# Fifteen matmuls of ones, results unread, in three waits of TensorE ahead of the experts

## The reference

```python
def moe_swiglu(h, w_router, w1, w3, w2):
    logits = (h @ w_router).astype(jnp.float32)
    top_val, top_idx = lax.top_k(logits, TOP_K)          # 2 of 8 experts for each token
    probs = jax.nn.softmax(top_val, axis=-1)
    combine = jnp.sum(jax.nn.one_hot(top_idx, N_EXPERTS, dtype=jnp.float32) * probs[..., None], axis=-2)
    out = jnp.zeros_like(h)
    for e in range(N_EXPERTS):                           # 1024 -> 3584 -> 1024 each
        out = out + combine[..., e:e + 1] * swiglu(h, w1[e], w3[e], w2[e])
    return out
```

## Time and profile before

| | |
|---|---|
| three timed runs | median 2060.42 us, 2057.94 to 2065.71 |
| the profiled execution | 2065.84 us |
| its span, first to last instruction | 2064.0 us (1.84 us lie around it) |
| TensorE busy | 2024.1 us, 98% of the span |
| weight loads busy | 1729.1 us, 84% |
| VectorE, ScalarE busy | 1580.3 us (77%), 1249.8 us (61%) |
| chain that ended last | TensorE 91%, VectorE 5%, issue 2%, ScalarE 2% |
| mean granted TensorE clock | 0.991 |

### The profile page before, as it was taken

One profiled execution on the slowest core, in us unless ns is written; L12 is line 12 of the kernel. 1 busy time (PEld: TensorE's weight loads), 2 busy tenths in 40 slices (PEclk: granted clock), 3 DMA queues, 4 the chain that ended last, 5 costly groups with the idle time before them and its releaser, 6 DMA issues.

```text
span 2064.0 us, 28723 instructions
## 1 busy us (share of the span) xinstructions
PE 2024.1 (98%) x10749; PEld 1729.1 (84%) x10749; DVE 1580.3 (77%) x1218; ACT 1249.8 (61%) x1066; POOL 13.9 (1%) x21
## 2 busy tenths in 40 slices
PE   9999999999999999999999999999999999999998
PEld 8988878789998988888777888888888888888887
DVE  4777955765445777955767898898989889898987
ACT  4665455444334565455446777777777777777775
POOL 0000000000000000000000000000000000000000
PEclk9999999999999999999999999999999999999999
DMA  7532455345554532455348999999999999999996
GB/s 257 165 100 90 142 176 183 102 155 188 187 184 143 184 103 82 143 166 182 104 170 296 380 354 379 372 357 379 358 381 354 378 371 355 379 358 379 356 375 243
DMA packets 240765, 516.59 MB, mean 250 GB/s; under 512 B 11528, under 2 KB 34312, under 8 KB 240686
## 3 DMA queue, kind: packets, MB, share of 16 engines
q1 hardware_dynamic: 238274, 507.39, 69.4%
q0 software_dynamic: 2144, 7.88, 1.1%
q10 hardware_dynamic: 268, 0.22, 0.0%
HBM read 513.35 MB, written 2.12 MB: 250 GB/s over the span
## 4 chain that ended last, share of the span: by engine, by line
PE 91%; DVE 5%; issue 2%; ACT 2%; DVEq 0%; ACTq 0%
PE PS L480 27%; PE PS L482 26%; PE PS L481 26%; PE PS L564 7%; PE PS L1085 1%; ACT hi L1208 1%; PE PS L1048 1%; PE PS L802 1%; PE PS L716 0%; DVE lo L1707 0%; DVE t_n L1730 0%; DVE stat L2121 0%; PE PS L1036 0%; DVE b_gc L2040 0%; PE PS L671 0%
## 5 line engine op out<-in xcount | busy, mean ns | idle before, releaser
L1707 DVE TENSOR_TENSOR lo<-raw,hi 128x2048 fp32r<-128x2048 f32 x481 | 1095.9, 2290 | 300.1 <-ACT hi L1208 297.4
L1208 ACT ACTIVATE hi<-raw 128x2048 fp32r<-128x2048 f32 x481 | 919.7, 1915 | 317.1 <-PE PS L482 308.6
L480 PE MATMUL PS<-hi,e_hi 128*128 128x512 f32 x896 | 355.1, 396 | 1.4 <-DVE e_lo L1730 1.4
L482 PE MATMUL PS<-hi,e_lo 128*128 128x512 f32 x896 | 349.5, 390 | 0.0
L481 PE MATMUL PS<-lo,e_hi 128*128 128x512 f32 x896 | 349.0, 389 | 0.0
L480 PE MATMUL PS<-hi,actT_hi 128*128 128x512 f32 x640 | 253.9, 397 | 3.7 <-DVE lo L1707 3.1
L482 PE MATMUL PS<-hi,actT_lo 128*128 128x512 f32 x640 | 249.6, 390 | 0.0
L481 PE MATMUL PS<-lo,actT_hi 128*128 128x512 f32 x640 | 249.1, 389 | 0.0
L480 PE MATMUL PS<-hi,fT_hi 128*128 128x512 f32 x536 | 208.7, 389 | 0.0
L482 PE MATMUL PS<-hi,fT_lo 128*128 128x512 f32 x536 | 208.7, 389 | 0.0
L481 PE MATMUL PS<-lo,fT_hi 128*128 128x512 f32 x536 | 208.6, 389 | 0.0
(11 more groups left out here) (332 smaller groups left out, 2128.7 us busy)
## 6 DMA issues: line engine op xcount, KB each, us to landing
raw<-in_moe_w SPq DMA_DIRECT2D x336, 1024.0 KB, 6.2
raw<-in_w_in SPq DMA_DIRECT2D x92, 1024.0 KB, 5.1
raw<-in_ffn_w SPq DMA_DIRECT2D x33, 1024.0 KB, 5.3
raw<-in_w_br SPq DMA_DIRECT2D x12, 1024.0 KB, 5.0
raw<-in_w_out SPq DMA_DIRECT2D x8, 1024.0 KB, 5.0
hankel<-hankel_dram POOLq DMA_DIRECT2D x1, 1536.0 KB, 9.9
x<-in_x SPq DMA_DIRECT2D x2, 512.0 KB, 5.4
f_gain<-in_norm_ffn POOLq DMA_DIRECT2D x2, 512.0 KB, 3.8
```

The lines of the kernel that those rows point to most:

```text
L480: pe.matmul(out, a_hi, b_hi, start=first, stop=False, skip_group_check=True)
L482: return pe.matmul(out, a_lo, b_hi, start=False, stop=last, skip_group_check=True)
L1208: act.activation(hi[prog.u % SPLIT][:, :], raw[slot][:, :], COPY).then_inc(hi_made.sem, 1)
L1707: dve.tensor_tensor(lo[prog.u % RAW][:, :], raw[prog.u % RAW][:, :], hi[s][:, :].bitcast(F32), ALU.subtract).then_inc(lo_made.sem, 1)
```

## The change

A helper `keep_awake(count)` issues `count` matmuls of ones by ones with 128 columns into bank 3 of PSUM. Nothing reads the result, and the next real product that uses the bank writes it anew. Seven stand behind the last `route`, ahead of the wait for `r_sel`; four behind the five counting matmuls, ahead of the wait for `pick`; four behind the gather, ahead of the wait for `e_lo`. The two groups of four are in the first turn of the experts only. No wait, signal, transfer or other instruction changes.

```diff
--- before.py
+++ after.py
@@ -1155,13 +1155,22 @@
             if turn:
                 pe.wait_ge(s_read.sem, s_read.count(2 * E * turn))
             n = E * turn
+            if turn == 0:
+                keep_awake(4)
             gather(n)
+            if turn == 0:
+                keep_awake(4)
             expert(n, 0, turn, True, False)
             with prog.loop(pe, PAIRS - 1, 0, rounds=2 * EXPERT_R) as i:
                 for s in (1, 0):
                     expert(i * 2 + (n + 2 - s), s, turn, False, False)
             expert(n + E - 1, 1, turn, False, True)
             scatter_last(n + E - 1, turn)
+
+        def keep_awake(count):
+
+            for _ in range(count):
+                mm(PS[:, 3, 0:P], ones, ones)
 
         def moe():
             pe.wait_ge(router_made.sem, 1)
@@ -1170,6 +1179,7 @@
             turn_x(1, 1)
             for half in range(2):
                 route(1, half)
+            keep_awake(7)
 
             pe.wait_ge(r_sel.sem, 2)
             mm(PS[:, 1, 0:E], le, r_t[:, 12, 0:E])
```

## The result

Over 20 executions each the changed kernel took 2066.14 us in the median (2060.16 to 2071.39), the kernel before 2061.1 us (2057.94 to 2066.2). The ratio is 1.002, with a 95% interval of 1.0012 to 1.0029: slower by about 4 us, where 2.9 us less were forecast. The profiled execution took 2070.31 us with a span of 2068.5 us; that of the kernel before had 2064.0.

A forecast was written before the change was run, and what follows sets the result against it. TensorE (98% busy) was taken as the bound, with its routing at half clock. Of 0.92 us (counting matmuls) plus 2.46 us (gather), 2.9 us was taken: 2060.42 - 2.9 = 2057.5 us, range 2053.8 to 2062.8 us.

The forecast's parts named there:

- The step that failed: From routing to kernel end: expert 0 starting a microsecond earlier ends the kernel about a microsecond earlier if transfers follow.
- Cost at full speed: 0: Ones in TensorE's three routing waits: at full clock all are covered by the gaps, costing 0.
- the sign: In the experts: what would show the forecast wrong, an earlier expert 0 offset by TensorE idle time; no size given.
- The gain in the routing: TensorE's path to expert 0: a clock that stays up saves 2.9 us, out of at most 3.38 us.
- The 0.92 us of the counting matmuls: Five counting matmuls at full clock: VectorE begins on their result at about 1078.79 instead of 1079.71, 0.92 us sooner.
- the four fifths of the gather's 2.46 us: Gather: full clock would save 2.46 us of its 5.28 us at half speed; four fifths of that was taken.
- the upper end: Routing: clock up throughout the counting matmuls and gather, expert 0 starting 3.38 us earlier, at 1085.1.
- The fall before the seven: Routing: clock falls before the ones start but returns sooner, gain 1.0 to 1.6 us, taken 1.2, 2059.2 us; chance 0.27.
- The blockade: Routing: half-speed ones delay the gather without bringing the clock back, 0.5 to 1.1 us slower, 2061.3 us; chance 0.13.
- the 22 matmuls of the warm-up: Kernel start: 22 matmuls of ones read as taking 4.77 to 9.59 us, giving 0.22 us each at full speed.
- No change by over 0.5%: Whole kernel: time neither faster nor slower by over 0.5%; chance 0.93.
- The range: Whole kernel: measured time between 2053.8 and 2062.8 us, widened for run-to-run spread.

The follow-up runs named there:

- e2: The kernel before, without ones, with TensorE's loop over expert pairs starting at place 181 of its fetch block; experts took 975.6 us, no total time given.
- i2: The kernel before with fifteen more matmuls of ones in the warm-up at the start (37 instead of 22), none in the routing; 2075.75 us, four executions timed.
- i1: The changed kernel with eleven, four and four ones as single 512-column matmuls, loop at no set place; expert 0 at 15.0 us behind the last product, no total given.
- e4: The changed kernel plus a hint to TensorE's sequencer each turn that the pair loop's jump back will be taken; expert 0 at 17.7 us, no total given.
- j1: The changed kernel with eleven ones behind the last route, four ahead of the gather, none behind it, as single 512-column matmuls, no set place; ratio 0.9991.
- e3: The kernel before with the pair loop's first instruction at place 32 of its block, control for the placing; as before, no total given.
- e1: The changed kernel, all ones kept, with the pair loop's first instruction at place 32 of its block; 2060.51 us, ratio 0.9997.
- f5: The changed kernel with each of the fifteen ones a single 512-column matmul of two instructions, loop at no set place; 2059.29 us, ratio 0.9985.

## Why the prediction was wrong

**The step that failed** is the one that carries the gain to the end: "Whoever starts expert 0 a microsecond earlier therefore ends the kernel about a microsecond earlier, provided the transfers follow", together with "Cost at full speed: 0". The transfers did follow. What I priced of the fifteen matmuls was their time on the array; that they are also 60 instructions ahead of a loop, and that the loop's place has a price, stood nowhere, not among the rivals either. It cost 6.1 us in the profiled execution, 2.0 at the first return of the loop and 4.1 at the second, where the clock fell too. In e2 and i2 the gaps are there without any ones in the routing. The prediction named the sign, "an earlier expert 0 with idle time of TensorE in the experts in its place", and had no mechanism for it. What the earlier trace rows show could not tell of it, since the loop fitted before; the row of q8 with its 55 packets, and the lack of any from 1400 to 1900 us, stood in the profile, and the loop returns in those very 500 us.

**The gain in the routing** was 2.1 us where I took 2.9. The 0.92 us of the counting matmuls came nearly as worked out: VectorE began at 1078.65 (forecast 1078.79), but its two `pick` took 0.74 us instead of 0.48, and the gather started 0.8 us sooner. Mis-sized was the four fifths of the gather's 2.46 us: the clock held through the seven but not into the gather, and 3.4 us at half speed remained; it took 1.3 us less instead of 2.0. i1 shows that the upper end could be had, 3.2 us against 3.38 worked out, but with eleven ones where the change has seven.

**The fall before the seven** exists as the rival had it: in e4 and j1 the clock fell at 3.3 us and the ones ran at half speed. Its gain was 1.4 us in e4 (19.1 to 17.7), forecast 1.2. The rival took its return of the clock, 3.4 us sooner than before, from no row; in e4 the clock came back 13.6 us behind the last product, in e3 17.0 us, which is just that. The blockade, ones at half speed that only cost, was seen in no run.

**A reading to correct**: I took the 4.89 us of 31 records for the 22 matmuls of the warm-up. The group began at 1.84 us and the stretch shown cuts it; in truth 22 matmuls took 7.75 us there, 0.35 us each, and the stretch that I divided by 22 holds 31 records, about 15 of them. That 0.22 us came out was luck; the seven, at 0.23 us, confirm the number and not the way to it.

**No change by over 0.5%**, the case with most of the chance, held: 0.2%. The range, which ended at 2062.8 us, did not hold the 2066.14.

Not settled: where exactly the limit lies and why it is below the place that a count of the body gives, why i1 misses at one return of two, why some placed loops have a gap at their entry, and how the hint does away with all fetches in the later turns.

## What to carry to other kernels

Instructions that cost an engine no time can still cost time by standing ahead of a long loop: before and after such an edit, compare the packets of the instruction queue, over the stretch of the loop, and look for gaps just behind its jumps back. Keep filler work in few instructions, or hint the jump. Ones in a wait can hold TensorE's clock or bring it back sooner: in the routing here 0.4 to 3.2 us, and 1.4 to 1.9 us even where they ran at half speed and delayed the work behind them.

## What the runs showed of the hardware

- A loop body of some 1886 TensorE instructions (by my count) is kept between turns when its first one lies at place 32 of a block of 256 (e1, e3) and is fetched anew in each turn at 100, 160, 168 and 181. In all returns that miss, but for i2's, TensorE goes on 2.9 to 3.1 us after a fetch of 16 KB has started, and the last 1.4 to 2.3 us of that are idle; in i2 the idle time is 3.2 and 3.3 us. It costs more where the clock falls in or just behind the gap and is down for 3.4 or 6.8 us.
- The kernel's own spread comes from the clock's timing. In the profile of the kernel before, the clock is down ahead of the routing for 10.2, 6.8 and 6.8 us, in e3's three times for 3.4 us, and the last product of `mixer(1)` ends at 1070.3 and 1063.4 us: 13.7 us less at half speed and 6.9 us sooner. In the rounds of the experiments every execution of the kernel before with a mean granted clock of 0.991 took 2064.4 to 2066.6 us, and those with 0.993 to 0.995 took 2057.8 to 2062.2. Executions of one kernel lie in groups about 5 us apart, so differences of 1 to 3 us are read inside the profile, from a common mark, rather than from the totals.
- The fifteen matmuls of 512 columns in the rounded type did for the clock what the float32 ones of 128 columns did, with half the instructions: routing 16.0 us in f5, 16.2 in the changed kernel, both with the fall at 8.5 to 8.9 us.
